# Two halves of 256 tokens in the matrix memory of a two-block transformer kernel

## The reference, cut to what matters

```
def step(carry, inp):                  # chunks of tokens, one head
    C, n, m = carry
    qj, kj, vj, ij, fj = inp
    b = jnp.cumsum(fj, axis=-1)
    a = b + m[..., None]
    D = jnp.where(lower, b[..., :, None] - b[..., None, :] + ij[..., None, :], -jnp.inf)
    m_t = jnp.maximum(a, jnp.max(D, axis=-1))
    w_inter = jnp.exp(a - m_t)
    s = jnp.einsum('bhtd,bhsd->bhts', qj, kj) * jnp.exp(D - m_t[..., None])
    num = jnp.einsum('bhts,bhsv->bhtv', s, vj) + w_inter[..., None] * jnp.einsum('bhvd,bhtd->bhtv', C, qj)
    den = jnp.sum(s, axis=-1) + w_inter * jnp.einsum('bhd,bhtd->bht', n, qj)
    h = num / jnp.maximum(jnp.abs(den), jnp.exp(-m_t))[..., None]
```

## Time and profile before

| | |
|---|---|
| three timed runs | 2057.3, 2059.47, 2065.16 us; median 2059.47 |
| span of the profiled execution | 2057.0 us; its own time is not listed apart, the nearest timed run is 2057.3 |
| TensorE busy | 2010.6 us, 98% of the span |
| VectorE, GpSimd, ScalarE busy | 1199.0, 906.8, 752.2 us |
| the stage of the matrix memory's heads | 1524.4 to some 1652.5 us of the span |

### The profile page before, as it was taken

One profiled execution on the slowest core, in us unless ns is written; L12 is line 12 of the kernel. 1 busy time (PEld: TensorE's weight loads), 2 busy tenths in 40 slices (PEclk: granted clock), 3 DMA queues, 4 the chain that ended last, 5 costly groups with the idle time before them and its releaser, 6 DMA issues.

```text
span 2057.0 us, 25915 instructions
## 1 busy us (share of the span) xinstructions
PE 2010.6 (98%) x10087; PEld 1672.1 (81%) x10087; DVE 1199.0 (58%) x1955; ACT 752.2 (37%) x1029; POOL 906.8 (44%) x500
## 2 busy tenths in 40 slices
PE   8999899999999999999999999999999899999998
PEld 6877788988888888877788788888888788888887
DVE  6454657646789895688578877516656752111112
ACT  5344534333513222447542122125353344222121
POOL 3422424754445444346244444445454345444442
PEclk9999999999999999999999999999999999999999
DMA  4322203516577862240348778423341023322321
GB/s 152 102 84 82 77 2 102 165 62 155 146 195 180 200 168 83 82 138 21 87 120 203 187 182 199 128 73 113 103 127 61 21 83 103 103 89 96 103 92 72
DMA packets 227823, 233.41 MB, mean 113 GB/s; under 512 B 6891, under 2 KB 222772, under 8 KB 227580
## 3 DMA queue, kind: packets, MB, share of 16 engines
q1 hardware_dynamic: 227216, 231.72, 40.1%
q10 hardware_dynamic: 492, 0.12, 0.0%
HBM read 229.56 MB, written 2.24 MB: 113 GB/s over the span
## 4 chain that ended last, share of the span: by engine, by line
PE 88%; DVE 7%; issue 2%; ACT 1%; DMA 1%; POOL 1%; SPq 0%; DVEq 0%; ACTq 0%
PE ps L2440 22%; PE ps L2442 21%; PE ps L2441 21%; PE ps L2491 7%; PE ps L2496 3%; DVE adacc L1985 2%; PE ps L3287 1%; PE ps L3273 1%; PE ps L2946 1%; PE ps L2877 1%; POOL wL L660 1%; PE ps L2728 1%; PE ps L2907 1%; DVE ssum L1478 1%; DMA raw<-in_w_in_dram 0%
## 5 line engine op out<-in xcount | busy, mean ns | idle before, releaser
L660 POOL TENSOR_TENSOR wL<-raw,wH 128x1024 fp32r<-128x1024 f32 (+2 forms) x320 | 769.3, 2425 | 948.7 <-ACT wH L839 883.6
L839 ACT ACTIVATE wH<-raw 128x2048 fp32r<-128x2048 f32 (+2 forms) x160 | 300.8, 1880 | 433.3 <-PE ps L2442 331.4
L2440 PE MATMUL ps<-uH,wH 128*128 128x512 f32 x1088 | 425.5, 391 | 3.0 <-DVE uL L1528 0.9
L2442 PE MATMUL ps<-uH,wL 128*128 128x512 f32 x1088 | 423.5, 389 | 0.0
L2441 PE MATMUL ps<-uL,wH 128*128 128x512 f32 x1088 | 423.4, 389 | 0.0
L1985 DVE SCALAR_TENSOR_TENSOR adacc<-adaw,adab,adacc 128x256 f32<-128x256 f32 x372 | 307.6, 827 | 12.9
L2440 PE MATMUL ps<-hnH,wH 128*128 128x512 f32 x728 | 287.7, 395 | 2.2 <-DVE xT L1597 1.7
L2442 PE MATMUL ps<-hnH,wL 128*128 128x512 f32 x728 | 283.8, 390 | 0.0
L2441 PE MATMUL ps<-hnL,wH 128*128 128x512 f32 x728 | 283.2, 389 | 0.0
L2440 PEld LDWEIGHTS ps<-uH,wH 128*128 128x128 f32 x1088 | 204.2, 188 | 46.9 <-issue 3.4
L2442 PEld LDWEIGHTS ps<-uH,wL 128*128 128x128 f32 x1088 | 204.2, 188 | 43.0
(11 more groups left out here) (478 smaller groups left out, 3035.3 us busy)
## 6 DMA issues: line engine op xcount, KB each, us to landing
raw<-in_ffn_w_dram SPq DMA_DIRECT2D x60, 1024.0 KB, 5.4
adaw<-in_ada_w_dram SPq DMA_DIRECT2D x192, 256.0 KB, 7.1
raw<-in_w_dram SPq DMA_DIRECT2D x32, 1024.0 KB, 5.5
raw<-in_w_in_dram SPq DMA_DIRECT2D x14, 1024.0 KB, 5.3
raw<-in_od_w_in_dram SPq DMA_DIRECT2D x12, 1024.0 KB, 5.3
raw<-in_w_xkv_dram SPq DMA_DIRECT2D x16, 512.0 KB, 3.6
raw<-in_ffn_w_dram SPq DMA_DIRECT2D x8, 768.0 KB, 4.2
raw<-in_ev_w_in_dram SPq DMA_DIRECT2D x5, 1024.0 KB, 5.3
```

The lines of the kernel that those rows point to most:

```text
L660: nc.gpsimd.tensor_tensor(wL[n % 2][:, k0:k1, 0:c], raw[n % 2][:, k0:k1, 0:c], wH[n % 2][:, k0:k1, 0:c].bitcast(F32), ALU.subtract).then_i ...
L839: nc.scalar.activation(wH[n % 2][:, 0:kc, 0:c], raw[n % 2][:, 0:kc, 0:c], ACT.Copy).then_inc(w_hi, 1)
L2440: nc.tensor.matmul(out_ap, wh, xh, start=first, stop=False)
L2442: return nc.tensor.matmul(out_ap, wl, xh, start=False, stop=last)
```

## The change

The 512 tokens are taken as two halves of 256. Scores, weights and their products are made only within a half. What the first half gives to the second (forwards), and the second to the first (backwards), goes through a state: keys times weights, times values, a 64x129 matrix per head and direction. The core of the diff:

```diff
@@ helpers @@
+    def half_range(d, j):
+        lo = j // 2 * 2 * P
+        return (j * P, lo + 2 * P) if d == 0 else (lo, (j + 1) * P)
@@ SP @@
-            sp.wait_ge(rows_out, 32)
+            sp.wait_ge(r_em, 3)
+            sp.dma_start(erows[:, 2 * P:S], Erow[0:ML_H, 2 * P:S]).then_inc(rows_out, 16)
+            sp.dma_start(erows[:, 0:2 * P], Erow[32:32 + ML_H, 0:2 * P]).then_inc(rows_out, 16)
+            sp.wait_ge(rows_out, 64)
+            sp.wait_ge(r_em, 5)
             sp.wait_ge(r_tr, 2)
...
+                if s == 3:
+                    sp.wait_ge(c_y, KC)
+                    (8 broadcasts of erows rows into decayed_queries(p))
@@ ScalarE, ahead of output_gate(0) @@
             nc.scalar.activation(erow[:], erow[:], ACT.Exp, scale=-1.0).then_inc(r_em, 1)
+            act.wait_ge(r_rows, 2)
+            nc.scalar.activation(Erow[0:ML_H, 2 * P:S], Mrow[0:ML_H, 2 * P:S], ACT.Exp, bias=rcol[0:ML_H, 0:1]).then_inc(r_em, 1)
+            (the same for the other direction)
+            act.wait_ge(r_tr, 1)
+            nc.scalar.activation(irow[0:ML_H, 0:2 * P], irow[0:ML_H, 0:2 * P], ACT.Exp,
+                                 bias=Mrow[0:ML_H, 2 * P - 1:2 * P]).then_inc(r_em, 1)
+            (the same for the other direction)
             output_gate(0)
             output_gate(1)
             high(n + 9)
...
+            act.wait_ge(r_tr, 3)
+            (two copies into wcol, each r_cols + 1)
@@ ScalarE, the loop over heads @@
+            gate_weights(0)
+            for h in range(ML_H):
+                if h + 1 < ML_H:
+                    gate_weights(h + 1)
+                states_copy(h)
                 if h in (0, 3, 5):
                     high(n + 11 + h // 2)
                 if h >= 2:
+            def states_copy(h):
+                hp = (h % 2) * 64
+                if h >= 4:
+                    act.wait_ge(l_o, 2 * (h - 4) + 2)
+                act.wait_ge(h_sp, HG_H + h + 1)
+                nc.scalar.activation(cst_[hp:hp + 64, h // 2 % 2, :, :], ps[3][hp:hp + 64, 0:2 * (ML_V + 1)]..., ACT.Copy).then_inc(h_st, 1)
@@ VectorE @@
+            for p in range(ML_H // 2):
+                keys_weighted(p)
+            queries_decayed(0)
+                    if x == 7 and h in (0, 2, 4):
+                        queries_decayed(h // 2 + 1)
@@ TensorE, after unit n+9 @@
+            pe.wait_ge(r_em, 5)
+            for tb in range(TB):
+                ins = nc.tensor.transpose(ps[4][:, tb * 64:(tb + 1) * 64], irow[:, tb * P:(tb + 1) * P], ident[0:64, 0:64])
+            ins.then_inc(r_tr, 1)
             pe.wait_ge(blk_taken, TAKEN[V_FILL[0]])
-            pe.wait_ge(r_cols, 2)
+            pe.wait_ge(r_cols, 4)
...
+                    if across:
+                        if i % 2 == 0:
+                            pe.wait_ge(l_kq, ML_H // 2 + h // 2 + 1)
+                            pe.wait_ge(h_st, 3 * HG_H + h + 1)
+                        ins = nc.tensor.matmul(dst, decayed_queries(h // 2)[hp:hp + 64, i, :], cst_[hp:hp + 64, h // 2 % 2, d, :],
+                                               start=False, stop=True)
...
             for h in range(ML_H):
                 next(beside, None)
-                scores_half(h + 1, 0)
+                scores(h + 1, 0)
                 next(beside, None)
+                if h == 0:
+                    pe.wait_ge(l_kq, ML_H // 2)
+                states(h)
```

More of the change, by code:

```diff
@@ L385, in bass_block_pair @@
     hgain = place("hgain", [P, D], F32, AR + 49408)[0]
[L386 to L393, removed]
+    wt = [[place(f"wt{i}{j}", [P, (2 - j % 2 if i % 2 == 0 else j % 2 + 1) * P], F32,
+                 ULOFF + 3072 * i + 1536 * (j // 2) + (1024 if i % 2 == 0 else 512) * (j % 2))[0] for j in range(TB)] for i in range(4)]
+    cst_ = place("cst_", [P, 2, 2, ML_V + 1], F32, ULOFF + 12288)[0]
     cy = place("cy", [P, KC, S], F32, UHOFF)[0]
@@ L3265, in out_rows @@
                     pe.wait_ge(l_h, 2 * h + d)
-                if h % 2 == 0 and h and d == 0:
-                    pe.wait_ge(blk_taken, TAKEN[V_FILL[0] + h])
-                for i in range(TB):
-                    dst = ps[6 + i // 2][:, (i % 2) * 129:(i % 2) * 129 + 129]
-                    js = range(0, i + 1) if d == 0 else range(i, TB)
-                    for j in js:
-                        at = (i - j if d == 0 else i) * P
-                        ins = nc.tensor.matmul(dst, wt[(2 * h + d) % 4][j][:, at:at + P], vx[:, j, h, :],
-                                               start=(j == js[0]), stop=(j == js[-1]))
@@ L3275, in out_rows @@
-                ins.then_inc(l_o, 1)
+                for i in (0, 1, 2, 3) if d == 0 else (2, 3, 0, 1):
+                    dst = ps[6 + i // 2][:, (i % 2) * 129:(i % 2) * 129 + 129]
+                    js = range(i // 2 * 2, i + 1) if d == 0 else range(i, i // 2 * 2 + 2)
+                    across = i // 2 != d
+                    for j in js:
+                        at = (i - j if d == 0 else i % 2) * P
+                        ins = nc.tensor.matmul(dst, wt[(2 * h + d) % 4][j][:, at:at + P], vx[:, j, h, :],
+                                               start=(j == js[0]), stop=(j == js[-1] and not across))
+                    if across:
[4 more added lines that the diff above has]
+                                               start=False, stop=True)
@@ new lines, in out_rows, with states @@
+                ins.then_inc(l_o, 1)
+            def states(h):
+                hp = (h % 2) * 64
+                if h % 2 == 0 and h:
+                    pe.wait_ge(blk_taken, TAKEN[V_FILL[0] + h])
+                if h:
+                    pe.wait_ge(h_st, 3 * HG_H + h)
+                for d in range(2):
+                    for j in (2 * d, 2 * d + 1):
+                        ins = nc.tensor.matmul(ps[3][hp:hp + 64, d * (ML_V + 1):(d + 1) * (ML_V + 1)], weighted_keys(h // 2)[:, j, hp:hp + 64],
+                                               vx[:, j, h, :], start=(j == 2 * d), stop=(j == 2 * d + 1))
+                ins.then_inc(h_sp, 1)
@@ L3277, in _, with scores @@
             pe.wait_ge(c_silu, KC)
-            def scores_half(h, d):
+            def scores(h, half):
                 if h >= ML_H:
@@ L3300, in head_transposes @@
                 ins.then_inc(n_tr, 1)
-            scores_half(0, 0)
-            scores_half(0, 1)
+            scores(0, 0)
+            scores(0, 1)
+            for p in range(ML_H // 2):
+                key_transposes(p)
             beside = values_beside()
@@ L3312, in _ @@
                 out_rows(h, 0)
-                scores_half(h + 1, 1)
+                scores(h + 1, 1)
                 next(beside, None)
```

70 lines of the change are left out of this document (60 added, 10 removed).

## The result

The changed kernel takes 2069.93 us (median of 5 runs, 2068.84 to 2073.98), the kernel before 2057.73 in the same comparison: ratio 1.0058, 95% interval 1.0041 to 1.0075. Forecast were 2060.0 us within 2053 to 2068 and "no change", so the time lies above the range and the kernel is slower by just over half a per cent. The profiled execution has a span of 2067.1 us for 2057.0 before.

The account below looks back on a forecast made before the run. TensorE, busy 98% of the span, was taken as the bound, with VectorE setting the pace at the end. 8.5 + 2.5 + 0.1 - 3.1 - 6.2 - 1.3 = +0.5 us gave 2060.0 us, range 2053 to 2068.

Parts of the forecast that it names:

- TensorE's count stays at 20 and nothing changes: Steady heads, `out_rows`: 16 products instead of 20, `states` adds 4, so TensorE's time there was to stay unchanged.
- six periods: Between starts of `out_rows(h,0)` up to `out_rows(6,0)`: 4 x (-1.9) - 0.8 + 2.2 = -6.2 us.
- the 12.5 of the forecast: Steady head's period: from 14.4 to 12.5 us, as scores of 256 columns instead of 512 save 1.9.
- The GpSimd hold: Heads 3 and 5: late `low` delays diagonals and VectorE, period 13.6; -0.8 instead of -1.9, and +2.2.
- The rival without a hold: Periods 3 and 5: GpSimd delays nobody, they reach -1.9 and -0.9, 4.2 less, 2055.8 us; chance 0.12.
- The stall in front: Ahead of unit n+9: ScalarE waits for `r_tr`, delaying `high(n+9)` and `low(n+9)`; +8.5 us, the largest term.
- The rival without a stall: Ahead of unit n+9: the third exponential does not hold up `high(n+9)`; 8.5 and 2.5 fall away, 2049.0 us; chance 0.08.
- The clock behind it: After TensorE's idle time ahead of unit n+9: granted clock falls, bounds 0 and 3.4, taken as +2.5 us.
- Up to the first product of head 0: From unit n+9 to `out_rows(0,0)`: +0.1 behind the unit, then 9.4 us at full clock instead of 12.5, -3.1.
- The second fall that a rival set at the scores: Before head 0, at 64-row products and sixteen transposes: clock falls again, +3.4, 2063.4 us; chance 0.19.
- The tail: From `out_rows(6,0)` on: VectorE sets the pace, `out_rows(6,0)` 0.45 shorter, eight multiplies 0.8 less; -1.3 us.
- The late state copy: Every head: ScalarE's state copy makes TensorE wait 1.5 us, 12 us in all, 2072.0 us; chance 0.11.

Follow-up runs that it names:

- the regrouped kernel: Changed kernel with the products with the state side by side, so a direction's four 64-row records stand together: 2069.62 us, ratio 1.0067.
- the run with the earlier transposes: Changed kernel with the four transposes of `irow` moved from behind unit n+8 to behind unit n+7: 2060.13 us, ratio 1.0021.
- the run with idle products to the end: Changed kernel plus unread filler products on TensorE in head 6 and 14 more ahead of `out_rows(7,1)`: 2066.51 us, ratio 1.0043.
- the three repairs: Changed kernel with `irow`'s transposes behind unit n+7, state product over 128 rows and `high` ahead of `states_copy`: 2050.37 us, ratio 0.9961.
- without the look-ahead: Changed kernel with the weights of head h made in ScalarE's turn h, not a head early: 2069.91 us, ratio 1.0056.

## Why the prediction was wrong

**Failed: "TensorE's count stays at 20 and nothing changes".** This step carried most of the six periods' miss of 6.8 us. The count was right, the price of a record was not: 0.11 holds between records of one shape. Where the height changes, the step to the first record of the new height and the step behind it are 0.20 to 0.22 each. In a steady head the state products bring six more changes of height, at some 0.2 us, less the overlap with the scores: 0.95 us a head, measured with the state products at 128 rows. The period came to 13.99, and to 13.04 in that run.

The 0.54 between 13.04 and the 12.5 of the forecast can be placed in the rows too. A pair of scores takes 1.06 to the next piece (1559.27 to 1560.33 in the regrouped kernel) where I had 0.96: 1.91 for the pair before held the changes of height around it, and halving the columns does not halve those. `states` takes 1.03 (1569.59 to 1570.62) where eight records at 0.11 are 0.9. The last 0.2 lies on its two sides: 0.21 in place of 0.12 from the piece into `states`, and 0.22 in place of 0.11 between the first two records behind it (1570.62 to 1570.83). So a change in the number of weight columns, 64 for 128, costs as a change of height does; no run tests this by itself. The trace of before held the hint: its scores are 64 rows between 128-row work, and I had priced them by the column.

**The GpSimd hold** came in time, but not by the wait that was forecast. 13.6 was forecast for both held periods, 14.14 and 14.18 came, and with TensorE quicker 13.99 and 14.22. GpSimd's times were right: the first diagonal of head 6 is ready 8.7 us after the start of `out_rows(5,0)`, for 8.85. But VectorE never waited for it. It was itself 0.95 us later, held up by its two stretched operations, which take 2.7 us more than before. By an estimate from these rows, without the stretch VectorE would have been ready at 1619.7 and would have waited until 1621.4. So about 1.8 us of delay would have come from the late diagonals anyway, and up to 0.95 is added by the stretch, a term that the prediction put at nothing. Both follow from the late `low`. In the changed kernel the hold costs next to nothing from 3 to 4, as the slow TensorE covers it, and 2.6 against before from 5 to 6 (+2.2 forecast; the period before was 11.58, from 1609.02 to 1620.60 by the timeline, not 11.4). Turning the order on ScalarE takes 1.8 of that away. The rival without a hold is refuted.

**The stall in front** was right in each link: 8.46 us for 8.5. The table load took its 1.28 us with the next row 0.01 behind it, as in the earlier trace rows. The page "ScalarE: Activation LUTs" of the Trainium skill (What ACT_TABLE_LOAD costs) would have made the gap 9.9; this trace does not show the drain. The rival without a stall is refuted by the run with the earlier transposes.

**The clock behind it** was mis-sized: +2.5 forecast, 1.4 left beside the gap, since about half of the fall lies in the gap (granted clock 0.53 from 1515 to 1520, where TensorE starts again at 1518.98).

**Up to the first product of head 0** -3.0 was forecast (0.1 - 3.1), and the run without the stall gives -2.8. The second fall that a rival set at the scores did not come: 1.00 from 1532 to 1542, although sixteen transposes stand there. Its "eight products with 64 rows" before and "four" after were a miscount: both kernels have four products, eight records, here, and those of the changed kernel are half as wide. The Trainium skill's rule in "TensorE: Matmul & The Clock Gate" (PE-mode transpose), that transposes do not bring the full clock, is not contradicted by this, but it gave no fall here.

**The tail: -1.3 forecast, +3.9 measured.** The second term that failed, 5.2 us. I took VectorE as the pace and the clock as given. The changed kernel reaches head 6 with TensorE idle for 2.88 us ahead of `states(6)`, and its clock falls. At the low clock (1.2 GHz) both `out_rows` of head 6 take 4.67 us, for 2.60 at full clock in the run with idle products to the end, and VectorE waits behind it: 4.19 us ahead of the denominators at 1631.59. At least 2.9 of the 3.9 is shown to be the clock. The last 1.0 is not settled, but that run's trace points at the idle products themselves: VectorE's readout of `out_rows(6,1)` ends at 1638.76, while TensorE, busy without a gap from 1633.71 with the idle products in its queue, starts `out_rows(7,0)` only at 1640.28. The forecast gain of 1.3 came in no run of the changed kernel; with the three repairs the tail is 0.8 shorter than before (28.1 for 28.96).

**The late state copy** in every head, the rival on the slow side, did not happen: TensorE is busy for all 13.99 us of head 1 in the changed kernel, and without the look-ahead the period stays 13.99. The time came out near that rival's 2072.0 for other reasons.

The sum of the misses: front -1.0, periods +6.8, tail +5.2, and the stage's earlier start -1.3, together 9.7; the measured span (2067.1) less the forecast one (2057.5) is 9.6.

## What to carry to other kernels

Price a short matmul by what stands beside it: when a change splits a contraction into 64-row products between 128-row ones, count the changes of height, and try the full height with zeros in the unused rows, or put products on opposite halves side by side. When an instruction is moved ahead in a queue, follow what its new wait holds up on that engine; a release one unit earlier was worth 9.9 us of span here, nearly all of the 10.1 between the two kernels. Where an engine's idle time drops its clock, removing one gap may move the fall to the next; read the clock by window in every run before a time is taken as a verdict. And where a wait was forecast and the time comes out right, look at the row: the engine may have been busy and not waiting, as VectorE was here.

## What the hardware showed that I had not expected

A change between 64 and 128 rows costs about 0.2 us of TensorE at these sizes, and 64-row products on opposite halves of the rows ran at once (starts 1558.78 and 1558.79).

Tiny operations of VectorE stretched beside GpSimd's work, as in the held period shown above. L2443 there ends at 1619.99 and L1563 at 1621.20, GpSimd's `low` and `gated_head` at 1619.96 and 1621.18. In the kernel with 128 rows it is the next two in line, L1563 with 2.26 us and L1564 with 1.21:
```profile
1586.69 2.26 DVE L1563 TENSOR_TENSOR adab<-small 128x4 f32<-128x4 f32 x1
1588.99 1.21 DVE L1564 SCALAR_TENSOR_TENSOR adab<-adab 128x4 f32<-128x4 f32 x1
```
They take 0.16 us elsewhere. In the traces of all twelve kernels, between 1520 and 1660 us, 52 operations of VectorE on two or four columns take over 0.3 us, and each ends within 0.04 us of the end of a tensor_tensor of GpSimd. The readouts from PSUM ran at their usual length beside the same `low`: 0.16 us for L2420 at 1615.37 in the changed kernel. What makes the one kind stretch and the other not is not tested by a run.
